# A hybrid attention layer on one core: the attention's v from products of 512 columns, and new orders for the engines

## What is computed

```
mod = silu(c) @ ada_w + ada_b;  shift, scale, gate = split(mod, 3)
h = rmsnorm(x, pre_norm_w) * (1 + scale) + shift
proj = h @ w_in       # mq mk mv mg (512 each), dq dk dv dz (512 each), db da (4 each)
o_moba = attention(rope(mq), rope(mk), mv) * silu(mg)     # 8 heads of 64, causal within 256 tokens
qkv = silu(short_conv([dq, dk, dv]))                      # 4 taps along the tokens
o_dn = rmsnorm(gated_delta_rule(qkv, g(da), sigmoid(db)), dn_norm_w) * silu(dz)   # 4 heads, chunks of 64
y = [o_moba, o_dn] @ w_out
out = x + gate * rmsnorm(y, post_norm_w)
```

## Time and profile before

| what | us |
|---|---|
| median of 3 runs | 201.45 (200.59 to 201.94) |
| the profiled execution, device time | 201.38 |
| its span, first to last instruction | 199.2 |
| PE busy / DVE busy / ACT busy / POOL busy | 185.7 / 138.4 / 104.1 / 83.4 |
| mean granted clock of TensorE | 0.988 |

### The profile page before, as it was taken

The page is one execution under the profiler, slowest core; times in us unless marked ns, Lnnn a source line. Parts: engine busy times, 40 slices in busy tenths (PEclk is TensorE's granted clock), DMA queues, the critical chain, the costliest instruction groups (busy, mean ns, idle before and its releaser), DMA issues.

```text
span 199.2 us, 4716 instructions
## 1 busy us (share of the span) xinstructions
PE 185.7 (93%) x1898; PEld 170.3 (86%) x1898; DVE 138.4 (69%) x326; ACT 104.1 (52%) x201; POOL 83.4 (42%) x46
## 2 busy tenths in 40 slices
PE   7999779999999989999999999997999999899970
PEld 6897769999999989988989999896999987588850
DVE  0638989463079988979878646746989399837364
ACT  2835445636398869396553226385234548337230
POOL 2037709795969616928065003974000220504000
PEclk9988999999999999999999999999999999999998
DMA  5999999999106530197308400062029357910022
GB/s 211 394 403 404 409 396 407 400 406 408 42 0 207 175 147 0 44 396 305 105 3 273 151 3 3 3 212 106 3 74 412 151 205 223 359 59 0 3 107 105
DMA packets 11527, 38.43 MB, mean 193 GB/s; under 512 B 1393, under 2 KB 1521, under 8 KB 10994
## 3 DMA queue, kind: packets, MB, share of 16 engines
q1 hardware_dynamic: 11362, 37.61, 50.6%
q10 hardware_dynamic: 144, 0.52, 0.7%
HBM read 37.08 MB, written 1.05 MB: 191 GB/s over the span
## 4 chain that ended last, share of the span: by engine, by line
PE 51%; DVE 28%; DMA 8%; ACT 6%; issue 3%; POOL 1%; DVEq 0%; SPq 0%; ACTq 0%; POOLq 0%
PE bank L1337 11%; PE bank L1338 10%; PE bank L1339 10%; DVE cv L951 7%; DVE accg L1139 5%; DMA raw<-in_w_out 4%; PE bank L1348 4%; DVE bank L926 3%; DMA outb<-in_post_norm_w 3%; PE bank L1547 3%; PE bank L1558 3%; PE bank L1535 2%; DVE pr L1114 2%; ACT whi L544 1%; DVE ssq L1003 1%
## 5 line engine op out<-in xcount | busy, mean ns | idle before, releaser
L471 POOL TENSOR_TENSOR wlo<-raw,whi 128x1024 fp32r<-128x1024 f32 (+1 forms) x25 | 57.4, 2317 | 66.7 <-ACT whi L544 66.7
L1337 PE MATMUL bank<-hhi,whi 128*128 128x256 f32 x224 | 65.3, 292 | 3.0 <-DVE hlo L895 2.1
L1338 PE MATMUL bank<-hhi,wlo 128*128 128x256 f32 x224 | 63.6, 284 | 0.0
L1339 PE MATMUL bank<-hlo,whi 128*128 128x256 f32 x224 | 63.5, 283 | 0.0
L1337 PEld LDWEIGHTS bank<-hhi,whi 128*128 128x128 f32 x224 | 43.1, 193 | 5.2 <-DVE hlo L895 2.9
L1338 PEld LDWEIGHTS bank<-hhi,wlo 128*128 128x128 f32 x224 | 43.2, 193 | 0.0
L1339 PEld LDWEIGHTS bank<-hlo,whi 128*128 128x128 f32 x224 | 43.1, 193 | 0.0
L544 ACT ACTIVATE whi<-raw 128x1024 fp32r<-128x1024 f32 (+1 forms) x33 | 33.0, 1026 | 10.6 <-PE bank L1339 7.5
L951 DVE SCALAR_TENSOR_TENSOR cv<-bank,convh,cv 128x255 f32<-128x255 f32 (+2 forms) x36 | 17.0, 481 | 8.6 <-ACT cv L608 7.6
L926 DVE SCALAR_TENSOR_TENSOR bank<-ada,sml,bank 128x512 f32<-128x512 f32 (+1 forms) x24 | 16.5, 687 | 0.7
L485 POOL TENSOR_TENSOR rot<-rot,cst 128x512 f32<-128x512 f32 x4 | 4.4, 1091 | 22.3 <-DVE rot L1081 20.4
(11 more groups left out here) (203 smaller groups left out, 359.0 us busy)
## 6 DMA issues: line engine op xcount, KB each, us to landing
raw<-in_w_rest SPq DMA_DIRECT2D x20, 512.0 KB, 5.1
ada<-in_ada SPq DMA_DIRECT2D x12, 512.0 KB, 8.7
ada<-in_gate_w SPq DMA_DIRECT2D x4, 1024.0 KB, 8.3
raw<-in_w_out SPq DMA_DIRECT2D x8, 512.0 KB, 6.2
ada<-in_ada SPq DMA_DIRECT2D x8, 256.0 KB, 6.1
raw<-in_w_qkv SPq DMA_DIRECT2D x5, 384.0 KB, 7.7
qkvs<-in_w_qkv SPq DMA_DIRECT2D x4, 384.0 KB, 9.2
cv<-in_w_qkv SPq DMA_DIRECT2D x4, 384.0 KB, 13.6
```

The lines of the kernel that those rows point to most:

```text
L471: pool.tensor_tensor(split_u(wlo, n), raw_u(n), split_u(whi, n).bitcast(F32), ALU.subtract).then_inc(lo_done, 1)
L1337: pe.matmul(out, a[0][ia], b[0][ib], start=start, stop=False, skip_group_check=skip)
L1338: pe.matmul(out, a[1][ia], b[0][ib], start=False, stop=False, skip_group_check=skip)
L1339: return pe.matmul(out, a[0][ia], b[1][ib], start=False, stop=stop, skip_group_check=skip)
```

## The change

The v columns of the attention are no longer two groups of 256 columns but one of 512, still over all eight k. Four units (`WIDE`, j = 6 to 9) hold two k each with 512 columns. `wide(j)` multiplies them with a token tile of h as stationary operand, 512 columns moving, into one whole bank per token tile; the first of the four waits for both bulk banks (`bulk_bank_free` for u = 3 and u = 4). `v_copy(i)` now copies a token tile's bank, and `pv` waits for both. `used_up` counts one more `unit_done`. The second halves of q and k are now groups 5 and 6.

`DVE_LO` changes: DVE takes the remainders 11, 12, 13, 14, 21 and 43 (before: 21, 34, 35, 37, 38, 41, 42, 43); POOL takes the rest. And the written orders of all five engines are new; the diff below shows of them what stands around the groups. Of the late DVE list, `gate_sums(0, 0, 4)` moves ahead of `maxima(1)` and `gate_sums(0, 4, 8)` ahead of `normalise(2)`; `gate_sums(1, 4, 8)` stands between `maxima(3)` and `normalise(3)`.

```diff
-GROUPS = [MQ, MK, MG, MV, MQ + 256, MK + 256, MV + 256, MG + 256, DZ, DZ + 256]
+GROUPS = [MQ, MK, MG, MV, MV, MQ + 256, MK + 256, MG + 256, DZ, DZ + 256]
+WIDE = (6, 7, 8, 9)
-        GQK = {0: (qT, 0), 1: (kT, 0), 4: (qT, 2), 5: (kT, 2)}
-        GV = {3: 0, 6: 1}
+        GQK = {0: (qT, 0), 1: (kT, 0), 5: (qT, 2), 6: (kT, 2)}
+        GV = {3: 0, 4: 1}
         GG = {2: (gm, 0), 7: (gm, 2), 8: (gz, 0), 9: (gz, 2)}
-        DVE_LO = (21, 34, 35, 37, 38, 41, 42, 43)
+        DVE_LO = (11, 12, 13, 14, 21, 43)
...
-                return (unit_done, N1 - 2 + j // 2 + 1) if j % 2 == 0 else (group_ready, j // 2 + 1)
-            return unit_done, N1 - 2 + N2 // 2 + j - N2 + 1
+                if j % 2 == 0 or j in WIDE[:-1]:
+                    return unit_done, N1 - 2 + sum(i % 2 == 0 or i in WIDE[:-1] for i in range(j + 1))
+                return group_ready, j // 2 + 1
+            return unit_done, N1 - 2 + N2 // 2 + 1 + j - N2 + 1
...
-                act.activation(vt[:, :, i * 256:(i + 1) * 256], two(bank_of_group(u)), ACT.Copy).then_inc(v_copied, 1)
+                act.activation(vt[:, i, :], bank[bank_of_group(u)][:, :], ACT.Copy).then_inc(v_copied, 1)
...
+            def wide(j):
+                n = N1 + j
+                if j == WIDE[0]:
+                    for u in GV:
+                        bulk_bank_free(u)
+                pe.wait_ge(*low_part(n))
+                for kk in range(2):
+                    k = 2 * (j - WIDE[0]) + kk
+                    for t in range(NT):
+                        ins = three(bank[bank_of_group(VS[t])][:, :], h_parts, w_parts, (slice(None), k, slice(t * P, (t + 1) * P)),
+                                    (slice(None), n % SPL, slice(kk * 512, (kk + 1) * 512)), start=(k == 0), stop=(k == NK - 1))
+                        if k == NK - 1:
+                            ins.then_inc(group_ready, 1)
+                if j != WIDE[-1]:
+                    ins.then_inc(unit_done, 1)
...
-                pe.wait_ge(v_copied, 1 if m < 2 else 2)
+                pe.wait_ge(v_copied, NT)
```

More of the change, by code:

```diff
@@ L1222, in _ @@
             modulate(3)
+            mod_sums(4, 2, 4)
+            ba_lo()
             h_lo(3)
-            mod_sums(4, 2, 4)
             mod_sums(4, 4, 8)
             modulate(4)
-            ba_lo()
+            lo(11)
             h_lo(4)
+            lo(12)
+            lo(13)
+            lo(14)
             conv(0)
@@ L1232, in _ @@
             conv(3)
+            conv_silu(0)
             gates_in()
+            conv_silu(1)
             rope(0)
-            conv_silu(0)
-            conv_silu(1)
+            conv_silu(2)
             gates_out()
-            conv_silu(2)
+            rope(1)
+            cum_copy()
             conv_silu(3)
-            cum_copy()
             lo(21)
-            rope(1)
+            conv(4)
+            conv(5)
+            conv_silu(4)
+            conv_silu(5)
+            gate(0)
             sum_squares(0)
@@ L1246, in _ @@
             sum_squares(3)
-            conv(4)
-            conv(5)
-            conv_silu(4)
+            maxima(0)
             columns()
-            conv_silu(5)
-            gate(0)
+            normalise(0)
             row_sum(0)
-            maxima(0)
             k_tokens(0)
             row_sum(1)
-            normalise(0)
+            k_tokens(1)
             v_tokens(0)
-            k_tokens(1)
+            v_tokens(1)
             decayed(0)
@@ L1263, in _ @@
             mask_z(0, 0)
-            maxima(1)
-            v_tokens(1)
             mask_z(0, 1)
-            rope(2)
-            normalise(1)
             mask_z(1, 0)
@@ L1271, in _ @@
             merge(1, 0)
-            q_decayed(0)
             merge(1, 1)
+            gate_sums(0, 0, 4)
+            maxima(1)
+            rope(2)
+            normalise(1)
             mask_z(2, 0)
@@ L1751, in _ @@
             half(0)
+            half(1)
             ba_turn()
-            half(1)
             half(2)
             half(3)
-            cum()
             k_turn(0)
             k_turn(1)
+            cum()
             q_turn(0)
@@ L1762, in _ @@
             half(5)
-            half(6)
-            half(7)
             scores(0)
+            wide(6)
+            wide(7)
             rows(0)
-            half(8)
+            wide(8)
+            p_turn(0)
             rows(1)
-            half(9)
+            wide(9)
             v_turn(0)
             v_turn(1)
-            p_turn(0)
             kk_products(0)
@@ L1786, in _ @@
             x_products(1, 1)
+            t_turn(2, 0)
+            half(10)
+            half(11)
+            half(12)
             z_products(2, 0)
-            t_turn(2, 0)
             t_turn(2, 1)
@@ L1795, in _ @@
             z_products(3, 1)
+            p_turn(1)
             x_products(3, 0)
```

295 lines of the change are left out of this document (142 added, 153 removed).

## The result

The changed kernel takes 208.81 us (median of 4 runs, 208.60 to 210.41), against 201.14 us for the kernel before on the same chip: ratio 1.0395, 95% interval 1.0331 to 1.0459. It is slower, as forecast, but by 7.7 us instead of 3.4. The profiled execution took 208.6 us with a span of 206.8, so 1.8 us lie around the span.

The account below looks back on a forecast made before the run. PE's queue of products was taken as the bound, DVE second. Early loss less products' gain, 5.5, minus later relief 2.1 gave +3.4 us; 199.2 + 3.4 + 2.2 = 204.8 us, range 198.9 to 208.6.

Parts of the forecast that it names:

- The products, -0.5: v products on PE: 48 of 512 columns (11.0 us) replace 96 of 256 (11.5 us), gaining 0.5 us.
- `q_turn`, 76.9: Early stretch: `rope(1)` now precedes `conv_silu(3)` on DVE, so the fourth `conv_silu`, which `q_turn` waits for, ends at 76.9 us.
- The gate ready at 87.0: DVE's early list finishes `gate(0)` at 87.0 us if nothing is held up; `wide(6)` needs its bank.
- `lo(21)` meets POOL, +1.6: DVE's `lo(21)` held by a POOL remainder: 1.6 us taken, bounds 0 and 2.4; `wide(6)` then starts at 88.6.
- The wait of 2.5 us at `wide(6)`: PE reaches `wide(6)` at 84.5 and waits 2.5 us for the gate at 87.0, if nothing on DVE is held.
- The later relief, -2.1: Waits before `p_turn` (1.4 us) and the gate row (0.7) vanish as six remainders leave DVE and `gate_sums` move forward.
- Rival (c): Much slower: POOL's back-to-back remainders hold two scalings of `normalise(3)`, delaying `p_turn(3)`; +3.5, 208.3 us; chance 0.18.
- (a): Even: `lo(21)` meets nothing (-1.6) and small later slips vanish (-0.9); +0.9, 202.3 us; chance 0.24.
- (b): Faster: later relief from moving 6.8 us off DVE exceeds the early loss; 199.0 us; chance 0.16.
- (d): v products: 512 columns would cost two passes of 256; excluded beforehand by a 0.23 us row, given no chance.
- The edits costed at nothing: Loads before 58 us, `lo(11)` to `lo(14)` in DVE's idle time, and `mod(4)` one unit earlier: 0 us taken for each.

## Why the prediction was right or wrong

**The products, -0.5.** Right: 0.45 us at `scores(1)` where the early order was that of before, and 0.23 us a step in `wide`. With halves in their place the kernel was no faster.

**`q_turn`, 76.9.** Right, 77.14. **The gate ready at 87.0.** Right, 87.05, by DVE's list. **`lo(21)` meets POOL, +1.6.** It did not; the bound of 0 held, by 0.37 us, a matter of chance at this distance, and another run showed the meeting at 2.2. So `wide(6)` began at 87.15, the lower edge of 87.0 to 89.4, and the early loss was 3.83 where the working without the meeting gives 3.9. The wait of 2.5 us at `wide(6)` was only 0.75, because PE got there 1.9 us later than the 84.5 of the sum, most of it the half clock behind `q_turn`. That fall was named as a thing that would make everything cost more; here it cost nothing, since the gate was the later of the two.

**The later relief, -2.1.** This is the step that failed. Its first half was right: the waits before the third `p_turn` (1.2 us idle) and before the gate row (0.5) vanished, and the middle gave back 1.9 us, though only because it started late. But "six remainders leave DVE for POOL, and `gate_sums` move forward" was priced as relief alone, and brought +5.7 us behind `scores(3)`: 2.6 at `p_turn(3)`, 1.2 at `vnew_products(1)`, some 1.4 of half clock around the first, 0.5 of `state_products(0)` that now stands there, less the 0.5 of the gate row, and 0.5 in small slips. The sum of the prediction with the measured terms is 199.2 + 3.8 - 1.9 + 5.7 = 206.8, the span.

**Rival (c) was what happened.** Two scalings were held, at 2.45 us each, 4.3 us above undisturbed, and 2.6 us of it reached PE (the slack was 1.7, near the 1 to 1.5 taken). Its condition was too strict: `hi(36)` ended at 161.49, 0.36 us after the scalings had started at 161.13. Two of them were through by then, and the third started at 161.59, 0.02 us behind POOL's remainder. Its 208.3 us is 0.5 below what was measured. It had a chance of 0.18 because I thought the two might miss by tenths. Scalings some tenths later would have met POOL all the same, since it had four remainders in a row, 9.4 us, which could have been read from its new list; scalings 0.6 us earlier would have been through before POOL began (an estimate from their 1.01 us and the 0.44 us that they were ahead). Its 208.3 was reached by adding it to the forecast, though, with the meeting of `lo(21)` in it and without the clock and `vnew_products(1)`: two terms too few and one too many.

**Rivals (a) and (b)** fell with the relief they rested on, (a) although `lo(21)` did meet nothing. **(d)** is excluded again: 0.23 us a step.

**The edits costed at nothing** (loads, `lo(11)` to `lo(14)`, `mod(4)`) cost nothing: PE is busy 27.83 of 27.90 us from 30.3 to 58.2 against 27.89 in the earlier trace rows, and with both orders restored, `mod(4)`, `lo(11)` to `lo(14)` and the front's transfers left in, the time is that of before (loads 20 to 27 were back in the order of their numbers there).

Open: whether the early order of before would do without v ahead of the gate and without the loads in order, which was not run; and how much of the 1.4 us of half clock belongs to the wait before it, since one run had the same wait without it.

## What to carry to other kernels

When several engines run orders that were made for each other, price a change of order as a new schedule, engine by engine to the end, and not as relief for the engine that is given less: where work goes counts as much as where it leaves. A wait is undone where its queue is late, not where it shows; five changes at the step that stood won nothing, and in the late stretch the order and the remainders had to be undone at once before either showed a clear gain. Try the large old pieces back first (one stretch on all engines), and single steps only after that.

## What the runs showed of the hardware

- In the changed kernel two stops of PE of 2.4 and 2.6 us, in work that was nearly full otherwise, each had 3.4 us at the lower level (1.2 GHz) around their end. It is no rule: with `conv_silu(3)` moved forward the stop of 2.6 us had none, and a stop of 0.95 us had one; with the six remainders given back, 2.4 us before `q_turn` were followed by 11.7 us at 1.00. At the lower level a 256-column product took 0.21 us instead of 0.12.
- Back-to-back remainders on POOL (2.35 us each) hold successive small DVE scalings, one of 0.28 or 0.35 us to a remainder, so that each takes 2.45 us; where POOL ran a single remainder (2.39 and 2.48 us), one scaling was held. A DVE remainder that began 0.37 us before POOL's took 1.22 us, one that began 0.34 us after it 3.43 us.
